# A decoder step's MLP: the sample rows of the down product in full fp32, in two half-width tiles, first in each down step

## The reference

```
def sq_relu_mlp(x, w_up, w_down):
    return jnp.square(jax.nn.relu(x @ w_up)) @ w_down

# per layer, for prompt rows and sample rows:
x = layer_norm(ALPHA * x + sq_relu_mlp(x, w_up[layer], w_down[layer]), ln2_g[layer], ln2_b[layer])
```

## Time and profile before

| | |
|---|---|
| median of 3 runs | 3557.73 us (3553.72 to 3574.97) |
| profiled execution, its own time | 3552.15 us |
| its span | 3550.4 us |
| mean granted clock of TensorE over the span | 0.938 |
| TensorE busy, of the span | 3193.3 us, 90% |
| VectorE / ScalarE / GpSimd busy | 43% / 25% / 11% |
| matmuls at L2437 (`hidden`), three kinds | 3 × 1536, mean 329 to 330 ns |
| matmuls at L2450 (`down`), `dn` operands | 3 × 1080, mean 390 ns |
| adds at L2620 | 504, mean 685 ns |
| `f_up_raw` loads | 32 of 1 MB, 7.1 us to landing |
| `f_dn_raw` loads | 30 of 1 MB, 4.9 us to landing |

### The profile page before, as it was taken

One profiled execution on the slowest core, in us unless ns is written; L12 is line 12 of the kernel. 1 busy time (PEld: TensorE's weight loads), 2 busy tenths in 40 slices (PEclk: granted clock), 3 DMA queues, 4 the chain that ended last, 5 costly groups with the idle time before them and its releaser, 6 DMA issues. The chain is left out here.

```text
span 3550.4 us, 47156 instructions
## 1 busy us (share of the span) xinstructions
PE 3193.3 (90%) x18329; PEld 2679.4 (75%) x18329; DVE 1528.1 (43%) x3152; ACT 901.4 (25%) x1895; POOL 394.0 (11%) x323
## 2 busy tenths in 40 slices
PE   8999759999898896899999999499786999999996
PEld 4655538778686774899999998388576899999995
DVE  1343324533433664344444446355343344444447
ACT  1121113323223332222111113244232211122113
POOL 0000110100100132111000013200022100011004
PEclk9999679999999997999999999699788999999998
DMA  4000143153486873111111111310233110111111
GB/s 173 18 25 11 32 79 108 49 188 139 133 301 205 317 261 130 44 47 47 47 47 33 38 59 42 107 41 32 85 134 116 48 47 26 45 47 47 47 36 63
DMA packets 144110, 309.98 MB, mean 87 GB/s; under 512 B 24616, under 2 KB 68520, under 8 KB 142888
## 3 DMA queue, kind: packets, MB, share of 16 engines
q1 hardware_dynamic: 143976, 308.16, 25.9%
HBM read 266.16 MB, written 97.80 MB: 103 GB/s over the span
## 5 line engine op out<-in xcount | busy, mean ns | idle before, releaser
L2437 PE MATMUL f_ps_u<-f_xT_hi,f_up_hi 128*128 128x384 f32 (+1 forms) x1536 | 507.1, 330 | 23.5 <-DVE f_up_lo L2594 12.1
L2437 PE MATMUL f_ps_u<-f_xT_lo,f_up_hi 128*128 128x384 f32 (+1 forms) x1536 | 505.2, 329 | 0.0
L2437 PE MATMUL f_ps_u<-f_xT_hi,f_up_lo 128*128 128x384 f32 (+1 forms) x1536 | 505.2, 329 | 0.0
L2620 DVE TENSOR_TENSOR f_acc<-f_acc,f_ps_d 128x512 f32<-128x512 f32 (+1 forms) x504 | 339.8, 685 | 245.4 <-PE f_ps_d L2450 245.4
L2450 PE MATMUL f_ps_d<-f_dn_lo,f_hT_hi 128*128 128x512 f32 x1080 | 421.2, 390 | 0.0
L2450 PE MATMUL f_ps_d<-f_dn_hi,f_hT_hi 128*128 128x512 f32 x1080 | 421.2, 390 | 0.0
L2450 PE MATMUL f_ps_d<-f_dn_hi,f_hT_lo 128*128 128x512 f32 x1080 | 421.1, 390 | 0.0
L2608 DVE TENSOR_TENSOR f_hT_lo<-f_h,f_hT_hi 128x384 fp32r<-128x384 f32 (+1 forms) x192 | 150.5, 784 | 564.3 <-ACT f_hT_hi L2514 564.3
L2437 PEld LDWEIGHTS f_ps_u<-f_xT_hi,f_up_hi 128*128 128x128 f32 x1536 | 292.3, 190 | 26.6 <-issue 15.8
L2572 POOL TENSOR_TENSOR f_h<-f_h 128x384 f32<-128x384 f32 (+1 forms) x192 | 152.5, 794 | 1364.9 <-ACT f_h L2509 1364.9
L2437 PEld LDWEIGHTS f_ps_u<-f_xT_lo,f_up_hi 128*128 128x128 f32 x1536 | 292.4, 190 | 1.1
(11 more groups left out here) (423 smaller groups left out, 4727.1 us busy)
## 6 DMA issues: line engine op xcount, KB each, us to landing
f_up_raw<-in_w_up SPq DMA_DIRECT2D x32, 1024.0 KB, 7.1
f_dn_raw<-in_w_down SPq DMA_DIRECT2D x30, 1024.0 KB, 4.9
w_group<-in_w_in_ab SPq DMA_DIRECT2D x9, 2048.0 KB, 14.7
out<-in_cache_dil_kv SPq DMA_DIRECT2D x8, 2016.0 KB
w_m<-in_w_in_ab SPq DMA_DIRECT2D x4, 2048.0 KB, 15.8
g_xn<-in_x_prompt SPq DMA_DIRECT2D x16, 512.0 KB, 3.8
sp_keys<-in_cache_dil_kv SPq DMA_DIRECT2D x8, 1024.0 KB, 8.4
sp_keys<-in_cache_dil_kv SPq DMA_DIRECT2D x16, 512.0 KB, 9.0
```

Source lines behind the costliest of these rows:

```text
L2437: last = pe.matmul(ps_u[b % 3][:, 0:w], wp[:, k, f * P:(f + 1) * P], xp[:, k, t0:t0 + w], start=(k == 0 and q == 0), stop=(k == KT - 1 and ...
L2620: dve.tensor_tensor(a, a, d, ALU.add).then_inc(d_free.sem, 1)
```

## The change

The sample rows of the down product are no longer computed in three F32R passes on split operands but by plain fp32 matmuls on unsplit ones: the squared activations of the 64 sample tokens go unrounded into a new small buffer `hS`, and the weights are read from `dn_raw`. The stationary operand has 64 columns; the left column half goes to PSUM partitions 0 to 63 of one bank, the right half to partitions 64 to 127 of the next. The sample block comes first in each down part (banks 0 and 1), with the prompt tiles in banks 2 to 17, and the adds follow this order. GpSimd squares the 64 sample tokens of units 4 and 5 into `hS` ahead of the other 256; ScalarE and VectorE round and split only those 256. The padding of `hT` and its clearing are gone. SyncE waits for the sample block of down part i before it loads `dn_raw` anew. In the last down part the sample block is computed first for both groups, the second from `last_dn_raw`.

```
-        hT = [[sb(f"hT{i}_{x}", [P, FT, NPAD], F32R) for x in ("hi", "lo")] for i in range(2)]
+        hT = [[sb(f"hT{i}_{x}", [P, FT, SEQ], F32R) for x in ("hi", "lo")] for i in range(2)]
+        hS = [sb(f"hS{i}", [P, FT, NS]) for i in range(2)]
...
+        def split_width(b):
+            t0, w = unit(b)[1]
+            return min(w, SEQ - t0)
+
+        def down_out(par, b):
+            bank = ps_d[(par * DN + b) % 4]
+            return bank[:, :] if b >= 2 else bank[b * NS:(b + 1) * NS, :]
+
+        dn_raw_flat = dn_raw[:, :, :].rearrange("p f n -> p (f n)")
...
                     sp.wait_ge(up_lo.sem, up_lo.done(i))
                     load_up(i + 1)
                     sp.wait_ge(dn_lo.sem, dn_lo.done(i))
+                    sp.wait_ge(d_full.sem, d_full.done(i, 1))
                     load_dn(i + 1)
...
                 sp.wait_ge(last_lo, 1)
+                sp.wait_ge(d_full.sem, d_full.done(NFG - 2, 1))
...
+                def down_sample(bank_par, par, raw, starts, stops):
+                    for f in range(FT):
+                        lasts = [pe.matmul(down_out(bank_par, c), hS[par][:, f, :], raw[:, f * D + c * 512:f * D + (c + 1) * 512],
+                                           start=(starts and f == 0), stop=(stops and f == FT - 1)) for c in range(2)]
+                    return lasts
+
-                def down_part(n, par, b, weights, starts, stops):
-                    m, c = b // 2, b % 2
+                def down_part(bank_par, par, b, weights, starts, stops):
+                    m, c = b // 2 - 1, b % 2
...
                 def down(n, par):
                     pe.wait_ge(dn_lo.sem, dn_lo.done(n))
                     pe.wait_ge(h_lo.sem, h_lo.done(n, UP - 1))
-                    for b in range(DN):
+                    pe.wait_ge(d_free.sem, d_free.done(n, 1, back=4))
+                    for last in down_sample(par, par, dn_raw_flat, True, True):
+                        last.then_inc(d_full.sem, 1)
+                    for b in range(2, DN):
                         pe.wait_ge(d_free.sem, d_free.done(n, b, back=4))
-                        down_part(n, par, b, dn_flat, True, True).then_inc(d_full.sem, 1)
+                        down_part(par, par, b, dn_flat, True, True).then_inc(d_full.sem, 1)
...
                 hidden(NFG - 1)
                 pe.wait_ge(dn_lo.sem, dn_lo.done(NFG - 2))
-                for b in range(DN):
+                pe.wait_ge(d_free.sem, d_free.done(NFG - 2, 1, back=4))
+                down_sample(0, 0, dn_raw_flat, True, False)
+                pe.wait_ge(squared.sem, squared.done(NFG - 1, UP - 1))
+                pe.wait_ge(last_loaded, 16)
+                for last in down_sample(0, 1, last_dn_raw, False, True):
+                    last.then_inc(d_full.sem, 1)
+                for b in range(2, DN):
...
-                    if b == 0:
+                    if b == 2:
                         pe.wait_ge(h_lo.sem, h_lo.done(NFG - 1, UP - 1))
                         pe.wait_ge(last_lo, 1)
...
-                for par in range(2):
-                    for part in range(2):
-                        last = pool.memset(hT[par][part][:, :, NTOK:NPAD].bitcast(F32), 0.0)
-                last.then_inc(cleared, 1)
...
-                            w = unit(b)[1][1]
-                            hs = h[(par * UP + b) % 3][:, 0:w]
+                            w, ws = unit(b)[1][1], split_width(b)
+                            hs, hr = h[(par * UP + b) % 3][:, 0:ws], h[(par * UP + b) % 3][:, ws:w]
                             pool.wait_ge(relu_done.sem, relu_done.done(n, b))
+                            if ws < w:
+                                pool.tensor_tensor(hS[par][:, b % FT, :], hr, hr, ALU.mult)
                             pool.tensor_tensor(hs, hs, hs, ALU.mult).then_inc(squared.sem, 1)
...
                 def add(n, par, m, first=False):
                     rows = rows_of(m)
                     for c in range(2):
-                        b = 2 * m + c
+                        b = 2 * ((m + 1) % NTT) + c
...
-                    for m in range(NTT):
+                    for m in (NT, *range(NT)):
                         add(n, par, m, first)
-                        if m == 2 and more:
+                        if m == 1 and more:
                             rest(n + 2, up_raw, up, up_hi, up_lo)
                     rest(n + 1, dn_raw, dn, dn_hi, dn_lo)
...
+                add(NFG - 2, 0, NT)
                 for m in range(NTT):
-                    add(NFG - 2, 0, m)
-                    dve.wait_ge(d_free.sem, d_free.done(NFG - 2, 2 * m + 1))
+                    if m < NT:
+                        add(NFG - 2, 0, m)
+                    dve.wait_ge(d_free.sem, d_free.done(NFG - 2, 2 * ((m + 1) % NTT) + 1))
                     moments(dve, link, t[m % 2], rows_of(m), acc[0:rows_of(m), m, :], ln_ready)
```

More of the change, by code:

```diff
@@ L2322 @@
 NTOK = SEQ + NS
-NPAD = (NT + 1) * P
 TOK_CHUNKS = [(0, 384), (384, 384), (768, 320)]
@@ L2368, in mlp @@
         last_loaded, last_hi, last_lo = sem("last_loaded"), sem("last_hi"), sem("last_lo")
-        gb_loaded, step, cleared = sem("gb_loaded"), sem("step"), sem("cleared")
+        gb_loaded, step = sem("gb_loaded"), sem("step")
         t_full, t_free, x_split = sem("t_full"), sem("t_free"), sem("x_split")
@@ L2444, in hidden @@
                         hidden_unit(n, b)
-                def down_part(n, par, b, weights, starts, stops):
-                    m, c = b // 2, b % 2
+                def down_sample(bank_par, par, raw, starts, stops):
[5 more added lines that the diff above has]
+                    m, c = b // 2 - 1, b % 2
                     for f in range(FT):
                         for q, (hp, wp) in enumerate(split_passes((hT[par][0], weights[0]), (hT[par][1], weights[1]))):
-                            last = pe.matmul(ps_d[(n % 2 * DN + b) % 4 if isinstance(n, int) else (par * DN + b) % 4][:, :],
+                            last = pe.matmul(down_out(bank_par, b),
                                              hp[:, f, m * P:(m + 1) * P], wp[:, f * D + c * 512:f * D + (c + 1) * 512],
@@ L2472, in _ @@
                         x_transposes(n)
-                pe.wait_ge(cleared, 1)
                 with pe.Fori(0, NFG // 2 - 1) as i:
@@ L2479, in _ @@
                 pe.wait_ge(dn_lo.sem, dn_lo.done(NFG - 2))
-                for b in range(DN):
+                pe.wait_ge(d_free.sem, d_free.done(NFG - 2, 1, back=4))
[5 more added lines that the diff above has]
+                for b in range(2, DN):
                     pe.wait_ge(d_free.sem, d_free.done(NFG - 2, b, back=4))
-                    down_part(NFG - 2, 0, b, dn_flat, True, False)
-                    if b == 0:
+                    down_part(0, 0, b, dn_flat, True, False)
+                    if b == 2:
                         pe.wait_ge(h_lo.sem, h_lo.done(NFG - 1, UP - 1))
                         pe.wait_ge(last_lo, 1)
-                    last = down_part(NFG - 2, 1, b, last_dn, False, True)
+                    last = down_part(0, 1, b, last_dn, False, True)
                     last.then_inc(d_full.sem, 1)
@@ L2511, in round_hidden @@
                 def round_hidden(n, par, b):
-                    f, (t0, w) = unit(b)
+                    f, (t0, _) = unit(b)
+                    w = split_width(b)
                     act.wait_ge(squared.sem, squared.done(n, b))
@@ L2613, in add @@
                     for c in range(2):
-                        b = 2 * m + c
+                        b = 2 * ((m + 1) % NTT) + c
                         dve.wait_ge(d_full.sem, d_full.done(n, b))
-                        a, d = acc[0:rows, m, c * 512:(c + 1) * 512], ps_d[(par * DN + b) % 4][0:rows, :]
+                        a, d = acc[0:rows, m, c * 512:(c + 1) * 512], down_out(par, b)
                         if first:
```

## The result

| | median us | ratio to before, 95% interval |
|---|---|---|
| kernel before | 3557.06 (4 runs) | |
| changed kernel | 3637.53 (4 runs) | 1.0222 [1.0178, 1.0266] |

The change makes the kernel about 2.2% slower. The profiled execution of the changed kernel took 3634.0 us (span 3632.2), 81.9 more than the one of before (3552.15). The forecast was 3628.

The account below looks back on a forecast made before the run. TensorE was taken to bound the MLP steps. From 3552.15 us: matmuls −21.6, stall from the added wait +67.2, clock falls +33.6, last down part −2.6, giving 3628.8, taken as 3628; range 3585 to 3655.

Parts of the forecast that it names:

- What bounds the kernel: MLP steps of 48.20 us: TensorE busy throughout at full clock, so a microsecond of matmul removed is a microsecond gained.
- The matmuls: Sample block in each down part: 2.72 us removed, 1.95 added, 0.77 saved; −21.6 us in all.
- Small edits: GpSimd's separate squaring of 64 columns, +0.2 us, hidden; removed memsets give nothing; the adds keep their number.
- The added wait: SyncE's wait delays load_up behind it; up weights come late, TensorE stalls 2.4 us in 28 down parts: +67.2 us.
- The clock: TensorE's clock falls after three in four of the 28 stalls, 1.6 us each: +33.6 us.
- The Trainium skill's other rule: Only a longer idle gap is to be avoided, so clock term 0; rival of stall at full clock, 3595 us, chance 0.21.
- The last down part: Less matmul work gains nothing there; two sample adds move from VectorE's chain end to behind last_lo: −2.6 us, two layers.
- The sum: 3552.15 − 21.6 + 67.2 + 33.6 − 2.6 = 3628.8 us, taken as 3628; chance 0.60.

Follow-up runs that it names:

- e1: Changed kernel with SyncE's queue reordered: load_up(i+2) ahead of the wait for the sample block and of load_dn(i+1); 3538.9 us, ratio 0.9943.
- e4: Changed kernel, up load still late, VectorE's rest for the up weights moved behind the adds of row tile 4 instead of 1; 3526.76 us, ratio 0.990.
- e2: Kernel before plus only one line: SyncE waits for bank 1 of down part i before load_dn(i+1); 3642.4 us, ratio 1.0243.
- e3: Changed kernel plus nine useless 128x512 matmuls before bank 10 of each down part in the loop, keeping TensorE busy in the stall; 3600.63 us, ratio 1.0109.
- e8: Changed kernel plus three useless 128x512 matmuls before bank 17 of each down part in the loop, lengthening the step by 0.68 us; 3643.5 us, ratio 1.0229.
- e5: Changed kernel, up load still late, VectorE's rest moved behind the add of bank 6 instead of bank 5; 3564.61 us, ratio 1.0021.

## Why the prediction was right, point by point

- **What bounds the kernel.** Right. With the stall cured, TensorE is busy in all of a step again and the step shrinks by what its matmuls shrink (e1, e4).
- **The matmuls.** Right in kind, the size a little off: 0.63 to 0.64 us saved per step, not 0.77. The block costs 2.07 us: eight records run in pairs as L2042 and L528 had shown, but the first full-width matmul behind the tiles is followed only 0.33 us later (1591.42, 1591.75) instead of 0.227. I had charged the extra start for entering and not for leaving. That is 4 us in 28 steps.
- **Small edits.** Hidden, as said. GpSimd's 64 columns take 0.29 us.
- **The added wait.** Right in each link: `load_up` at T+3.1 (forecast 3.1), ScalarE at T+10.2 (10.2), VectorE at T+12.1 (12.15), TensorE at T+15.05 (15.25). A step without a fall is 49.89 us (49.8), so the stall costs 49.89 − 47.57 = 2.32 us (2.4); the profile shows 1.9 to 2.1 of it as idle, since the last matmul's record runs into it. e1, e2 and e4 show it as cause, by the queue, by the wait alone and by VectorE's order.
- **The clock.** The mechanism is shown by e3. The number of falls was a guess from four cases, three in four: 24 of 28 came, for 21 taken, each 1.5 us (51.40 − 49.89) for 1.6. That three in four was near was luck: e2 and e8 have 10 and 12 of 28 with stretches as long or longer. When a fall comes follows a beat of its own in the traces. In the changed kernel the first four falls begin at 1502.55, 1553.75, 1604.95 and 1656.15, 51.20 us apart, while TensorE resumes every 51.4 to 51.5 us, so from 0.8 us ahead of the fall to 0.2; all four stalls without a fall ended 0.1 to 0.3 us after the next such moment. In e8 the falls of a layer are 102.4 or 153.6 us apart, twice and three times as much. The Trainium skill ("TensorE: Matmul & The Clock Gate", What's actually happening) says that the activity is looked at in a rhythm that runs on by itself and is not restarted by the kernel. These moments agree with it, and so does e8's count, 12 instead of 24 for steps 0.7 us longer. The Trainium skill's other rule (same page, Why this matters for your kernels), by which only gaps longer than ours matter and which I had set against the rows, was contradicted: 24 gaps of 1.9 to 2.7 us were each followed by a fall, and e3 prices them at 37 us.
- **The last down part.** Half seen. Outside the 28 steps, which are 87.6 us longer, the profiled run is 5.8 us shorter (81.8 more in all). From the last down part's start VectorE's last product ends 2.5 us sooner in the second layer (75.2 us before, 72.6 after), where I had 1.3 a layer. The stretch from the first layer's last down part to the second layer's first is 3.1 us shorter, but it holds the stages between, and runs with the same code there differ by as much (631.0 to 634.4 us in e4 and e1). I had the adds moving, but not that the sample blocks fill the wait for `last_lo`; the clock at 1.00 behind it fits the rest of the gain, and no run tests it by itself.
- **The sum.** −17.9 for the matmuls (28 × 0.64), +65.0 for the stall (28 × 2.32), +36.2 for the clock (24 × 1.51), +4.3 that is left of the steps, mostly in the first and last of each loop, whose stalls were 2.5 to 2.7, −5.8 outside them: +81.8, for +76.6 forecast. The forecast had the gain 3.7 too large and the stall 2.2 too large, the clock 2.6 and the ends 3.2 too small, and nothing for the longer stalls at the ends of the loops. The errors have both signs and partly cancel.

## What to carry to other kernels

A wait added to an in-order queue delays whatever stands behind it; before adding one, follow the next instruction of that queue to its reader, and that reader's own queue to the engine that sets the pace. Here it was enough to issue the other load first, or to let VectorE reach its late operand three row tiles later: with either, the loss of 2.2% becomes a gain of 0.6 to 1.0%. And an idle stretch of an otherwise saturated TensorE can cost more than its length, for the clock may fall behind it.

## What the runs showed of the hardware

- **Same stall, different share of falls.** Idle stretches of mostly 1.9 to 2.1 us in steps of 49.9 us: 24 falls of 28; the same in steps of 50.6 us: 12; of 2.1 to 2.4 us in steps of 50.7 us: 10. The stretch's length alone does not say whether the clock falls. In e5 the one of 1.75 us was followed by a fall, four of 1.2 to 1.3 us and 23 of 0.5 to 0.8 us were not.
- **Two 64-column tiles on different PSUM partitions run fully side by side in fp32**: eight records in 1.94 us, against 3.65 on the same partitions.
- **The stages ahead of the MLP vary by themselves.** In the profiled runs, the first `up` matmul came at 1416.7 us before, at 1416.9 in the changed kernel and at 1436.6 in e1, whose code is the same up to there. Over those first 1400 us the records give TensorE a mean granted clock of 0.92, 0.92 and 0.91. e1's time of 3538.9 against e4's 3526.8 is within that size, which is why the steps in the trace and not the totals tell such kernels apart. What starts the difference stays open; no run was made for it.
